# Out-projection of a hybrid attention layer in 2x2 blocks with seven products instead of eight

## The reference

```python
h = rms_norm(x, g_in)
proj = h @ w_in
...
out_a = swa_sink_attention(qa, ka, va, a_sinks) * jax.nn.silu(a_gate)     # 16 heads of 64: 1024 wide
out_b = mla_attention(qb_nope, qb_rope, kb_nope, kb_rope, vb) * jax.nn.silu(b_gate)   # 512 wide
out_m = memory_cross_attention(qm, km, vm) * jax.nn.silu(m_gate)          # 512 wide
mixed = jnp.concatenate([out_a, out_b, out_m], axis=-1)
return x + mixed @ w_o                                                    # w_o: 2048 x 2048
```

## Time and profile before

| | |
|---|---|
| median of 3 runs | 1561.23 us (1561.17 to 1562.7) |
| span of the profiled execution | 1559.8 us |
| TensorE busy | 1509.3 us (97%) |
| VectorE, ScalarE, GpSimd busy | 599.2, 444.0, 111.5 us |
| mean granted TensorE clock | 0.990 of full speed |
| moved by DMA | 135.58 MB, mean 87 GB/s |

### The profile page before, as it was taken

The page is one execution under the profiler, slowest core; times in us unless marked ns, Lnnn a source line. Parts: engine busy times, 40 slices in busy tenths (PEclk is TensorE's granted clock), DMA queues, the critical chain, the costliest instruction groups (busy, mean ns, idle before and its releaser), DMA issues.

```text
span 1559.8 us, 17751 instructions
## 1 busy us (share of the span) xinstructions
PE 1509.3 (97%) x7088; PEld 1224.2 (78%) x7088; DVE 599.2 (38%) x831; ACT 444.0 (28%) x796; POOL 111.5 (7%) x84
## 2 busy tenths in 40 slices
PE   7999999999999999999998897999998999999998
PEld 6888888888888888888866686657778888888886
DVE  6633230524432222213166576775557222120202
ACT  6431312113131201111042555883447221010100
POOL 0110000202010000000001122010000000000000
PEclk9999999999999999999999899999999999999999
DMA  8121331121213121312134522440022314141301
GB/s 328 41 57 52 108 107 40 54 94 54 99 50 108 41 108 40 108 54 94 54 135 135 172 72 64 115 132 14 14 67 74 144 54 149 54 148 54 106 29 54
DMA packets 41743, 135.58 MB, mean 87 GB/s; under 512 B 4192, under 2 KB 8288, under 8 KB 41696
## 3 DMA queue, kind: packets, MB, share of 16 engines
q1 hardware_dynamic: 28240, 83.90, 16.4%
q0 software_dynamic: 13312, 51.03, 9.4%
q10 hardware_dynamic: 144, 0.02, 0.0%
HBM read 106.61 MB, written 28.32 MB: 87 GB/s over the span
## 4 chain that ended last, share of the span: by engine, by line
PE 91%; ACT 4%; DVE 2%; issue 2%; DMA 1%; POOL 0%; ACTq 0%; DVEq 0%; POOLq 0%
PE ps L1328 26%; PE ps L1329 26%; PE ps L1330 26%; PE ps L1531 2%; PE ps L1494 2%; PE ps L1495 2%; ACT a_p L733 2%; PE ps L1484 1%; PE ps L1512 1%; PE ps L1537 1%; PE ps L1498 1%; PE ps L1466 1%; PE ps L1509 1%; PE ps L1526 1%; DVE m_parts L1048 0%
## 5 line engine op out<-in xcount | busy, mean ns | idle before, releaser
L1328 PE MATMUL ps<-w_hi,h_hi 128*128 128x512 f32 x1152 | 449.1, 390 | 9.9 <-DVE h_lo L853 9.1
L1329 PE MATMUL ps<-w_lo,h_hi 128*128 128x512 f32 x1152 | 448.8, 390 | 0.0
L1330 PE MATMUL ps<-w_hi,h_lo 128*128 128x512 f32 x1152 | 448.6, 389 | 0.0
L842 DVE TENSOR_TENSOR w_lo<-w_raw,w_hi 128x1024 fp32r<-128x1024 f32 x121 | 151.7, 1254 | 747.7 <-ACT w_hi L564 747.5
L564 ACT ACTIVATE w_hi<-w_raw 128x1024 fp32r<-128x1024 f32 x121 | 127.9, 1058 | 902.9 <-PE ps L1330 895.8
L1328 PEld LDWEIGHTS ps<-w_hi,h_hi 128*128 128x128 f32 x1152 | 216.7, 188 | 55.2 <-issue 9.1
L1330 PEld LDWEIGHTS ps<-w_hi,h_lo 128*128 128x128 f32 x1152 | 216.7, 188 | 44.9
L1329 PEld LDWEIGHTS ps<-w_lo,h_hi 128*128 128x128 f32 x1152 | 216.7, 188 | 44.8
L1329 PE MATMUL ps<-h_lo,w_hi 128*128 128x512 f32 (+1 forms) x544 | 211.8, 389 | 0.0
L1328 PE MATMUL ps<-h_hi,w_hi 128*128 128x512 f32 (+1 forms) x544 | 211.7, 389 | 0.0
L1330 PE MATMUL ps<-h_hi,w_lo 128*128 128x512 f32 (+1 forms) x544 | 211.6, 389 | 0.0
(11 more groups left out here) (228 smaller groups left out, 1434.0 us busy)
## 6 DMA issues: line engine op xcount, KB each, us to landing
w_raw<-in_w SPq DMA_DIRECT2D x121, 512.0 KB, 3.3
gate_s<-T POOLq DMA_DIRECT2D x4, 2048.0 KB, 7.0
mixed<-gate_s POOLq DMA_DIRECT2D x16, 512.0 KB, 5.0
x_raw<-in_xT SPq DMA_DIRECT2D x7, 1024.0 KB, 18.2
aq_s<-T POOLq DMA_DIRECT2D x2, 2048.0 KB, 7.5
a_q_at<-aq_s SPq DMA_DIRECT2D x16, 256.0 KB, 3.8
S<-in_x POOLq DMA_DIRECT2D x2, 2048.0 KB, 10.0
T<-in_x POOLq DMA_DIRECT2D x2, 2048.0 KB, 12.7
```

Source lines behind the costliest of these rows:

```text
L842: v.tensor_tensor(w_lo[:, n % SPLIT, :], w_raw[:, n % RAW, :], w_hi[:, n % SPLIT, :].bitcast(F32), ALU.subtract).then_inc(lo_ready, 1)
L1328: mm(out, a_hi, b_hi, start=start, stop=False)
L1329: mm(out, a_hi, b_lo, start=False, stop=False)
L1330: return mm(out, a_lo, b_hi, start=False, stop=stop)
```

## The change

The out-projection is computed by Winograd's form of the 2x2 block product. Weights are stationary, the mixed activations move, so the result is transposed (`yT`, turned back on the host, and the residual comes from `xT`).

- Two passes (halves) over the contraction: rows 0 to 7 of `mixed` first, rows 8 to 15 after. In each, blocks are 512 tokens by 512 of the contraction (4 tiles, `NPAIR`) by 128 columns; 8 groups per pass cover 256 columns each: 16 groups (`NG`) in all. The first pass writes x plus its share to a scratch in HBM (`half_s`), the second reads it back instead of x.
- A group is seven products P1, P6, P7, P5, P2, P4, P3 of 4 x 3 = 12 matmuls, over three PSUM banks (two sets in turn). P5 and P3 are added in PSUM onto P6, P2 onto P1, P4 onto P7. VectorE empties banks between them: nine drains into four corner tiles (11, 12, 21, 22) of 128x512 that hold x.
- Per half, four sums of the left operand (128x2048 each: `left_sum`) and two of its low halves (`low_sides`) run on GpSimd, seven high halves on ScalarE (`high_left`), five low halves on VectorE (`low_left`). Per group, four sums of the right operand (128x512, `made_right`) and seven low halves (`low_right`, `LEAD` = 3 products ahead) run on VectorE, seven high halves on ScalarE (`high_right`, up to `RING` = 9 ahead).
- For the first half this starts inside attention M (`ahead`), whose loops are now written out. For the second half each left operand is renewed during groups 7 and 8, once its product of group 7 is done.
- SP issues all loads (1 MB of weights and four tiles of 256 KB per group), GpSimd the four stores per group. Corners 12 and 21 have two buffers, 22 and 11 one.

```diff
+NPAIR = 4
+P1, P6, P7, P5, P2, P4, P3 = range(7)
+OUT_G = D // OUT_COLS
+NG = 2 * OUT_G
+LEAD = 3
+RING = 9
...
 # SP
+            def load_right(G):
+                if G >= 2:
+                    sp.wait_ge(product_done, 7 * (G - 1))
+                sp.dma_start(wq[G % 2][:], io["w_out"][G]).then_inc(wq_loaded[G % 2], 16)
+
+            def load_x(G, corner):
+                k = x_slot(G, corner)
+                if x_turn(G, corner) >= 1:
+                    sp.wait_ge(xq_stored[k], 16 * x_turn(G, corner))
...
+            for G in range(1, NG):
+                for corner in (12, 21, 22, 11):
+                    load_x(G, corner)
+                if G + 1 < NG:
+                    load_right(G + 1)
...
 # GpSimd
+            def left_sum(half, part):
...
+                if half == 1:
+                    pool.wait_ge(product_done, 7 * OUT_G - 7 + (P1, P1, P6, P7)[part] + 1)
+                if part >= 1:
+                    pool.wait_ge(s_made, 4 * half + part)
+                out, x, y, op = ((s1, a21, a22, ALU.add), (a21, a11, a21, ALU.subtract), (s2, s1, a11, ALU.subtract),
+                                 (s4, a12, s2, ALU.subtract))[part]
+                g.tensor_tensor(out, x, y, op).then_inc(s_made, 1)
...
+            def low_sides(half):
+                raw, lo = left_raw(half), left_lo(half)
+                for j in (P2, P4):
+                    pool.wait_ge(a_hi_ready, 7 * half + j + 1)
+                    g.tensor_tensor(lo[j], raw[j], a_hi[j][:].bitcast(F32), ALU.subtract).then_inc(a_lo_pool, 1)
...
+            pool.wait_ge(B.gated, len(BSTEPS))
+            for part in range(4):
+                left_sum(0, part)
+            low_sides(0)
+            for G in range(NG):
+                turning = G == OUT_G - 1
+                if turning:
+                    left_sum(1, 0)
+                    left_sum(1, 1)
+                store(G, 22, "c22")
+                if turning:
+                    left_sum(1, 2)
+                store(G, 11, "c11")
+                store(G, 21, "c21")
+                if turning:
+                    left_sum(1, 3)
+                store(G, 12, "c12")
+                if turning:
+                    low_sides(1)
...
 # ScalarE
             def ahead(c):
+                if c == 2:
+                    high_right(P1)
+                    high_left(0, P1)
+                elif c == 4:
+                    high_right(P6)
+                    high_left(0, P6)
+                elif c == 5:
+                    high_right(P7)
+                elif c == 6:
+                    high_right(P5)
+                    high_left(0, P7)
...
+            for n in range(P3, 7 * NG):
+                for j in range(7):
+                    if n == 7 * OUT_G + (3, 6, 7, 8, 8, 8, 8)[j]:
+                        high_left(1, j)
+                high_right(n)
...
 # VectorE
+            def low_left(half, j):
+                dve.wait_ge(a_hi_ready, 7 * half + j + 1)
+                dve.wait_ge(s_made, 4 * half + (4 if j in (P6, P3) else 3))
...
             def ahead(c):
+                if c == 3:
+                    made_right(0, 1)
+                    made_right(0, 2)
+                elif c == 4:
+                    made_right(0, 3)
+                    made_right(0, 4)
+                    low_left(0, P1)
+                elif c == 5:
+                    low_first(P1)
+                elif c == 6:
+                    low_first(P6)
+                    low_left(0, P6)
+                elif c == 7:
+                    low_first(P7)
...
             gate(M, TT - 1, 1, TT // 2 - 1)
+            low_left(0, P7)
+
+            first_next = 7 * (OUT_G - 1) + P4
+            for n in range(7 * NG):
+                if n + LEAD < 7 * NG:
+                    low_right(n + LEAD)
+                if n == P1:
+                    low_left(0, P5)
+                if n == P7:
+                    low_left(0, P3)
+                drain_product(n)
+                if n - first_next in (0, 1, 2, 3, 5):
+                    low_left(1, {0: P1, 1: P6, 2: P7, 3: P5, 5: P3}[n - first_next])
...
 # TensorE
             pe.wait_ge(M.gated, TT)
+            for G in range(NG):
+                half, a_lo = G // OUT_G, left_lo(G // OUT_G)
+                for j in (P1, P6, P7, P5, P2, P4, P3):
+                    n = 7 * G + j
+                    if G % OUT_G == 0:
+                        pe.wait_ge(*lefts(half, j))
+                    pe.wait_ge(wp_lo_ready, n + 1)
+                    if j in (P1, P6, P7):
+                        if G >= 2:
+                            pe.wait_ge(drained, drains(G - 2, {P1: "c11", P6: "c12", P7: "c21"}[j]))
+                    else:
+                        pe.wait_ge(drained, drains(G, {P5: "u2", P2: "x22", P4: "c22", P3: "v"}[j]))
+                    bank = 3 * (G % 2) + {P1: 0, P2: 0, P6: 1, P5: 1, P3: 1, P7: 2, P4: 2}[j]
+                    first = j in (P1, P6, P7)
+                    for i in range(NPAIR):
+                        ins = three(ps[:, bank, :], wp_hi[n % RING][:, i, :], right_lo(n)[:, i, :],
+                                    a_hi[j][:, i, :], a_lo[j][:, i, :], first and i == 0, i == NPAIR - 1,
+                                    skip=not first)
+                    ins.then_inc(product_done, 1)
```

More of the change, by code:

```diff
@@ L176, in layer @@
         ident = small("ident", [P, P])
+        cos_at = top[0]
         cos = small("cos", [P, TT, 32])
@@ new lines, in low_sides, with store @@
+            def low_sides(half):
[3 more added lines that the diff above has]
+                    g.tensor_tensor(lo[j], raw[j], a_hi[j][:].bitcast(F32), ALU.subtract).then_inc(a_lo_pool, 1)
+            def store(G, corner, name):
+                pool.wait_ge(drained, drains(G, name))
+                k = x_slot(G, corner)
+                pool.dma_start(x_place(half_s if G < OUT_G else io["yT"], G, corner), xq[k][:]
+                               ).then_inc(xq_stored[k], 16)
@@ L548, in gate_sigmoid @@
+            for k in range(6):
+                pool.wait_ge(xq_stored[k], 16 * (NG // 2 if k < 4 else NG))
         def gate_sigmoid(act, a, group):
@@ L821, in _, with high_left @@
-            for c in range(1, CPG):
-                for k in (2 * c, 2 * c + 1):
-                    high_mixed(k)
-                high(CH_OUT + c)
-            for n in range(CH_OUT + CPG, NCH):
-                high(n)
+            def high_left(half, j):
+                if half == 0:
+                    act.wait_ge(B.gated, len(BSTEPS))
+                else:
+                    act.wait_ge(product_done, 7 * OUT_G - 7 + j + 1)
+                made = {P6: 3, P7: 2, P5: 1, P3: 4}
+                if j in made:
+                    act.wait_ge(s_made, 4 * half + made[j])
+                a.activation(a_hi[j][:], left_raw(half)[j], ACT.Copy).then_inc(a_hi_ready, 1)
@@ new lines, in _ @@
+            m_tiles = tiles_of(M, TT, beside=ahead)
+            for i in range(TT // 2):
+                m_tiles(i)
+            act.wait_ge(M.pv, TT)
+            high_left(0, P5)
+            high_right(P2)
+            high_left(0, P2)
+            high_left(0, P4)
+            high_right(P4)
+            high_left(0, P3)
+            for n in range(P3, 7 * NG):
[3 more added lines that the diff above has]
+                high_right(n)
@@ new lines, in low_left, with drain @@
+            def low_left(half, j):
+                dve.wait_ge(a_hi_ready, 7 * half + j + 1)
+                dve.wait_ge(s_made, 4 * half + (4 if j in (P6, P3) else 3))
+                v.tensor_tensor(left_lo(half)[j], left_raw(half)[j], a_hi[j][:].bitcast(F32), ALU.subtract
+                                ).then_inc(a_lo_ready, 1)
+            def drain(G, name, corner, bank):
+                k = x_slot(G, corner)
+                v.tensor_tensor(xq[k][:], ps[:, 3 * (G % 2) + bank, :], xq[k][:], ALU.add).then_inc(drained, 1)
@@ new lines, in drain_product @@
+            def drain_product(n):
+                G, j = n // 7, n % 7
+                if j == P7:
+                    return
+                dve.wait_ge(product_done, n + 1)
+                if j == P1:
+                    for corner in (12, 21, 22):
+                        dve.wait_ge(xq_loaded[x_slot(G, corner)], 16 * (x_turn(G, corner) + 1))
+                        drain(G, f"x{corner}", corner, 0)
+                elif j == P6:
+                    dve.wait_ge(drained, drains(G, "x21"))
+                    drain(G, "u2", 21, 1)
+                elif j == P5:
+                    dve.wait_ge(drained, drains(G, "x22"))
+                    drain(G, "v", 22, 1)
+                    dve.wait_ge(drained, drains(G, "v"))
+                    drain(G, "c22", 22, 2)
+                elif j == P2:
+                    dve.wait_ge(xq_loaded[x_slot(G, 11)], 16 * (x_turn(G, 11) + 1))
+                    drain(G, "c11", 11, 0)
+                elif j == P4:
+                    dve.wait_ge(drained, drains(G, "u2"))
```

(4 more changed lines are left out.)

231 lines of the change are left out of this document (147 added, 84 removed).

## The result

The changed kernel takes 1569.4 us (median of 7 runs), the kernel before 1562.24 beside it: ratio 1.0039, 95% interval 1.0027 to 1.005. It is slower by 0.4%, where I had forecast a gain of 0.5%. Its profiled span is 1567.7 us, 7.9 us longer than before. One of the seven runs was disturbed (2136 us) and stands outside the ratio.

A forecast was written before the change was run, and what follows sets the result against it. TensorE was taken as the bound, the out-projection costing exactly its matmuls. 1559.8 - 43.5 + 9 + 6 + 19 + 2 = 1552.3 us for the profiled span, 1553.7 median; range 1527 to 1576.

The forecast's parts named there:

- the turn: Groups 7 and 8, left operands renewed: +19 us under the lock, ends 7 and 25, plus 2 for clock.
- the end: After the last matmul: drain, store issue and landing keep their shape, last store 256 KB instead of 512; nothing counted.
- the lock: A streaming GpSimd operation holds up VectorE operations with two SBUF inputs for as long as it streams; PSUM drains are exempt.
- a slow GpSimd: Rival: GpSimd's operation takes longer than 4.7 us; half-way, 6.7 us, gives 1578, 8.8 us gives 1603; chance 0.17.
- What is removed: Out-projection: seven products instead of eight, 1344 matmuls instead of 1536 at 0.2268 us each, saving 43.5 us.
- the gain isn't there: Rival: 112 product boundaries cost something each, or the corner-22 tile comes late; 34 us at 0.3 us a boundary; chance 0.06.
- GpSimd's price: Each of GpSimd's twelve 128x2048 operations takes 4.7 us, scaled from its elementwise select over 128 columns.
- place 1: Memory attention ahead of the out-projection: VectorE's added work and held scalings cost +9 us, ends 2.6 and 12.
- the first three slip in between the scalings: Memory attention: three GpSimd sums fit between VectorE's softmax scalings, the next two late by 0.5 and 1.5 us, slack 2.6.
- Group 0: First out-projection group: VectorE's leftover low halves and GpSimd's two delay the fourth and sixth products, +6 us, ends 1.7 and 8.
- are earlier than VectorE's all the same: Groups 7 and 8: ScalarE's 7 x 1.92 us come before VectorE's steps despite ScalarE waiting for the third sum.
- the no-lock rival: Rival: sums stream fast or VectorE slips in between; 31.9 us gained, 1529.3 us; chance 0.27 with the cases in between.

The follow-up runs named there:

- the best kernel: Changed kernel with all twelve GpSimd operations on VectorE, the second half's sums made ahead, and the last group's four stores issued by SyncE: 1540.65 us, ratio 0.9851.
- the small kernel: Separate kernel without the computation: VectorE operations alone, then beside GpSimd additions of 128x2048; an addition of two SBUF tiles went from 0.70 to 4.9 us.

## Why the prediction was wrong

Its direction was wrong; its range (1527 to 1576) held the time. The forecast kept only 7.5 us of the 43.5, and the costs set against them came out 15.4 us higher. The largest share of that, 4.1 us, is attention M, where the step on how GpSimd's sums and VectorE's scalings take turns failed; the turn adds 3.1, the end 2.8, and no single one of them turns the sign alone. That the lock would matter was right, and my own forecast gave its being slower only 0.03: the 0.16 that I had on slower stood on a slow GpSimd. By its own steps:

- **What is removed** was right to the tenth: 1344 matmuls, 0.2268 us apart, and TensorE without a gap in the steady groups. The rival "the gain isn't there" is out; a group costs 0.07 to 0.19 us over, 1.9 us in all, and in these groups the 1 MB of weights and the single tile for corner 22 never came late.
- **GpSimd's price** was right, 4.5 us for 4.7 taken. So the rival that ends slower by a slower GpSimd is out too: slower came without it. The select was the right row to scale, and the all-reduce the wrong one; as the select has one input and the sum two, that the two prices agree so well is in part luck.
- **The lock** was right in kind. What failed in place 1 is the step "the first three slip in between the scalings", the next two of them late by 0.5 and 1.5 us. The first sum started 0.03 us ahead of a scaling and held it, and the next scaling ended 9.2 us late. With it failed the list of what is exposed: I wrote the scaling, the weight sums and the low halves, but the multiplication of four columns, one for each tile in attention M, is held too, twice by 3.1 us. Attention M cost 13.1 us where I took 9 (11.6 to 13.9 in all five traces with it), at or beyond my upper end of 12. That the GpSimd work alone does most of it is shown by the kernel before with four sums (8.8 us in its trace, 9.7 in its median). How much of the 4.1 us too few comes from the turns taken and how much from the four columns wasn't separated, nor was the rest, VectorE's and ScalarE's own added steps, which I had at 2.6. With no GpSimd operation at all attention M still costs 7.9 us (all twelve on VectorE), part of it the wait of 1.5 us for the first weights.
- **Group 0** was mis-sized by little: 7.4 for 6. I had counted no clock there, and after the second of its two gaps eight matmuls at up to 0.43 us cost 1.6 of it.
- **The turn**: 24.1 us for 19 + 2 (24.0 to 26.3 in four traces). The count (49.2 us of work through one lock against 29.9) was sound, and near the upper end. The step that failed is the sentence that ScalarE's high parts "are earlier than VectorE's all the same": the first came 21 us after it could. Taking that wait away gave nothing back, so ScalarE's order was a link and not the cause. What bound the turn was shown by moving the twelve to VectorE (14.4) and by starting two sums early (11.5, VectorE at 95%). The 7.3 us that I had for the turn without the lock were too few as well: 13.5 with GpSimd's operations cut to 8 columns. With that and attention M, the no-lock rival's 1529 us was out of reach: 1550.57.
- **The end** I had counted at nothing. It cost 2.8 us, and the reason isn't the landing: the last store lands 2.3 us after its issue where it had taken 3.9, yet GpSimd's last issue stands 8.7 us before the end where it had stood 5.9. Why its end is longer in the new kernel isn't known; six waits instead of one are ruled out.
- **Earlier stages**: 2.1 us that no step had. They are spread between executions and not the change. The scaling of attention M's first tile stands at 1163.45 to 1166.12 us in the thirteen traces, in both kernels: at 1163.45, 1164.57 and 1166.08 in the three of the kernel before, at 1163.50 in the best kernel.

The deeper mistake lies in the comparison that I didn't make. Place by place I asked what is lost with GpSimd's twelve operations under the lock and found 34 us, 11.6 of them without it, and did not ask the same with the twelve on VectorE, 27.4 us of its time at 2.28 each. For the turn the sum is short: 31.4 + 6 x 2.28 = 45.1 us of work against 29.9, +15.2 instead of +19, and 14.4 were measured. The rows for it were on the table.

## What to carry to other kernels

An operation given to GpSimd is not free because GpSimd is idle. Next to a VectorE that works mostly in SBUF it can cost VectorE up to its whole length (4.5 us here). So compare that first with what VectorE would need itself (2.28 here), and look whether VectorE reads PSUM meanwhile. When buffers change hands one by one, count the work of the busiest engine over that stretch, start what can be done in place before it, and only then mend orders. And look at who issues the last store: SyncE instead of GpSimd took 2.9 us off the end before the change and 6.5 after it. Before an edit is blamed for a longer wait, see whether a DMA that it doesn't touch came late in that one trace.

## What was not expected of the hardware

- A VectorE multiplication of 128x4 with one SBUF source, 0.17 us, took 3.24 us under a GpSimd addition, and 1.56 instead of 0.19 in the small kernel. A reduction and a reciprocal from SBUF kept their 0.69 and 0.18 us there.
- GpSimd's addition of 128x2048 took 4.5 us, and 5.4 where a VectorE operation was in first: the holding works both ways.
- From the issue of GpSimd's last store to the end of the span passed 8.6 to 8.8 us in the kernels with the new out-projection (9.2 with its operations cut to 8 columns, 5.9 in the kernel before), though the store had landed after 2.3. From SyncE's last store, where it issued all four, passed 2.4 us (3.3 in the kernel before).
- The first weights of the out-projection, 1 MB on SyncE's queue with nothing changed about them, took 4.7 to 5.0 us to land in eight traces, and 7.3 and 7.8 in two.
- With the same work and shorter but more numerous gaps (the kernel with ScalarE's order mended) TensorE lost 8.1 us to the 1.2 GHz level at the turn instead of 3.9 (3.9 to 5.3 in the four traces with the turn unchanged). In the changed kernel the granted clock was 0.65 over the ten us around the end of its longest gap.
